# Gate logits from split values in 96 stacked rows, and the last four mixing steps of block B in the last two ticks of the dense layer of block A

## The reference, cut to what matters

```python
h = rmsnorm(x, p['norm_mix_g'])
z = jnp.einsum('btd,de->bte', h, p['w_in'])          # D_IN columns, 16 of them are glr
gq, gk, gv, gg, glr, dq, dk, dv = jnp.split(z, _split_points(), axis=-1)
gate_logit = jnp.einsum('btr,rk->btk', glr, p['w_gk2']) + p['b_gk']
log_a = (jax.nn.log_sigmoid(gate_logit) / GK_NORMALIZER).reshape(B, T, H_GLA, DK_GLA)
...
mix = jnp.concatenate([o_g.reshape(B, T, -1), o_d.reshape(B, T, -1)], axis=-1)
x = x + jnp.einsum('bte,ed->btd', mix, p['w_out'])
h2 = rmsnorm(x, p['norm_ffn_g'])
u = jnp.square(jax.nn.relu(jnp.einsum('btd,df->btf', h2, p['w_up'])))
x = x + jnp.einsum('btf,fd->btd', u, p['w_down'])
```

## Time and profile before

| | |
|---|---|
| median of 3 runs | 1342.72 us (1342.07 to 1342.86) |
| the profiled execution, its own time | 1342.28 us |
| span of the profiled execution | 1340.1 us |
| TensorE matmul busy | 1331.6 us, 99% |
| VectorE busy | 896.2 us, 67% |
| ScalarE busy | 577.6 us, 43% |
| GpSimd busy | 395.8 us, 30% |
| granted TensorE clock | 1.0 as the mean of the span |

### The profile page before, as it was taken

One profiled execution on the slowest core, in us unless ns is written; L12 is line 12 of the kernel. 1 busy time (PEld: TensorE's weight loads), 2 busy tenths in 40 slices (PEclk: granted clock), 3 DMA queues, 4 the chain that ended last, 5 costly groups with the idle time before them and its releaser, 6 DMA issues.

```text
span 1340.1 us, 23935 instructions
## 1 busy us (share of the span) xinstructions
PE 1331.6 (99%) x8605; PEld 1123.7 (84%) x8605; DVE 896.2 (67%) x1619; ACT 577.6 (43%) x1078; POOL 395.8 (30%) x397
## 2 busy tenths in 40 slices
PE   9999999999999999999999999999999999999999
PEld 8788888777777777887777777677999999999998
DVE  6479667846757776767666674444566665887785
ACT  7464333425645563631424342232454354434532
POOL 3648434455515434341000000000522210332030
PEclk9999999999999999999999999999999999999999
DMA  9458744454365565676658565881665465133301
GB/s 330 125 182 227 238 144 139 141 173 132 98 202 191 179 213 171 215 253 219 236 181 300 181 240 177 294 285 69 213 206 185 162 220 174 48 111 111 111 33 64
DMA packets 126135, 240.33 MB, mean 179 GB/s; under 512 B 13673, under 2 KB 47258, under 8 KB 126018
## 3 DMA queue, kind: packets, MB, share of 16 engines
q1 hardware_dynamic: 116802, 214.68, 48.8%
q10 hardware_dynamic: 9216, 24.14, 5.4%
HBM read 198.16 MB, written 40.62 MB: 178 GB/s over the span
## 4 chain that ended last, share of the span: by engine, by line
PE 96%; DVE 3%; ACT 1%; issue 1%; ACTq 0%; POOL 0%; DVEq 0%; POOLq 0%
PE ps L87 26%; PE ps L89 25%; PE ps L88 25%; PE ps L1576 3%; PE ps L1613 2%; PE ps L1396 2%; PE ps L3424 2%; PE ps L1597 1%; PE ps L428 1%; PE ps L1811 1%; PE ps L490 1%; PE ps L491 1%; PE ps L1437 1%; PE ps L1438 1%; PE ps L452 1%
## 5 line engine op out<-in xcount | busy, mean ns | idle before, releaser
L3182 POOL TENSOR_TENSOR kr<-kr,qb 128x512 f32<-128x512 f32 x128 | 174.3, 1370 | 161.9 <-DVE sd L3167 110.5
L87 PE MATMUL ps<-x2hB,uw_h 128*128 128x264 f32 (+1 forms) x512 | 145.1, 283 | 0.1
L88 PE MATMUL ps<-x2lB,uw_h 128*128 128x264 f32 (+1 forms) x512 | 144.7, 283 | 0.0
L89 PE MATMUL ps<-x2hB,uw_l 128*128 128x264 f32 (+1 forms) x512 | 144.5, 282 | 0.0
L87 PE MATMUL ps<-part_h,fh 128*128 128x264 f32 (+1 forms) x448 | 127.8, 285 | 0.0
L89 PE MATMUL ps<-part_h,fl 128*128 128x264 f32 (+1 forms) x448 | 127.1, 284 | 0.0
L88 PE MATMUL ps<-part_l,fh 128*128 128x264 f32 (+1 forms) x448 | 126.9, 283 | 0.0
L2948 DVE TENSOR_TENSOR xt<-xt,ps 128x264 f32<-128x264 f32 (+1 forms) x224 | 87.4, 422 | 35.8 <-PE ps L89 35.6
L3167 DVE TENSOR_REDUCE sd<-kr 128x8 f32<-128x512 f32 x128 | 85.4, 677 | 35.0 <-POOL kr L3182 35.0
L87 PE MATMUL ps<-uh,dh 128*128 128x512 f32 x256 | 104.1, 406 | 0.9 <-DVE xt L2255 0.8
L87 PE MATMUL ps<-x2hA,uw_h 128*128 128x512 f32 x256 | 104.5, 408 | 0.0
(11 more groups left out here) (395 smaller groups left out, 3406.6 us busy)
## 6 DMA issues: line engine op xcount, KB each, us to landing
kr<-in_cache_k SPq DMA_DIRECT2D x128, 256.0 KB, 3.1
raw_up<-in_w_up_units SPq DMA_DIRECT2D x64, 512.0 KB, 4.1
vr<-in_cache_v SPq DMA_DIRECT2D x128, 256.0 KB, 4.5
raw_dn<-in_w_down SPq DMA_DIRECT2D x32, 512.0 KB, 6.1
raw_dn<-in_w_down ACTq DMA_DIRECT2D x32, 512.0 KB, 4.7
raw<-in_w_in_units SPq DMA_DIRECT2D x23, 512.0 KB, 5.5
raw_up<-in_w_out_units SPq DMA_DIRECT2D x16, 512.0 KB, 4.0
kept_up_low<-uw_l SPq DMA_DIRECT2D x14, 512.0 KB, 6.4
```

Of the source, the lines that this page charges most:

```text
L87: pe.matmul(out, lh, rh, start=first and n == 0, stop=False, skip_group_check=onto)
L88: pe.matmul(out, lh, rl, start=False, stop=False, skip_group_check=onto)
L89: ins = pe.matmul(out, ll, rh, start=False, stop=last and n == len(ks) - 1, skip_group_check=onto)
L3182: pool.tensor_tensor(k[:, :], k[:, :], qb[v // PAGES][:, :], ALU.mult).then_inc(k_multiplied, 1)
```

## The change

Two things are changed.

1. **The gate logits.** `low` becomes a tile of its own, 96 rows of type fp32r at the address of `dg`, whose rows 96 to 127 now take the 32 rows that `low_rank` makes. ScalarE (`low_highs`, at the end of group 11) copies the high part of these rows into rows 0 to 31 and 64 to 95 of `low`, and the high part of `wgk` into rows 0 to 31 and 32 to 63 of a new tile `wgk_r`: eight copies. VectorE (`low_lows`, in group 12, behind the low parts of weight pieces 8 and 9) makes rows 64 to 95 of `wgk_r` and rows 32 to 63 of `low`: four subtractions. One fp32r matmul over the 96 rows gives high by high, high by low and low by high at once, in place of one float32 matmul over 128 rows. Each of the six now waits for the low part of its own piece. Two small memsets on GpSimd and one wait of SyncE go.
2. **The mixing.** The last four steps of block B's mixing are put at ticks 142, 142, 143 and 143.

```diff
-    low = dg
+    low = at("low", 170.6875, [96, NT], FP32R)
+    wgk_r = at("wgk_r", 4.75, [96, 256], FP32R)
...
-                sp.wait_ge(sem("pool_steps"), 8)
                 sp.wait_ge(gcol_in, 16)
                 for i in range(2):
-                    sp.dma_start(m["wgk"][16 * i:16 * (i + 1), :], a["w_gk2"]).then_inc(gcol_in, 16)
+                    sp.dma_start(m["wgk"][96 + 16 * i:112 + 16 * i, :], a["w_gk2"]).then_inc(gcol_in, 16)
...
+            if g == START["low"] + 2:
+                low_highs(act)
...
-            step.note(pool.memset(low[:, SEQ:NT], 0.0))
...
-            step.note(pool.memset(m["wgk"][:, :], 0.0))
...
-            dve.tensor_tensor(low[0:32, c0:c0 + n], ps[0:32, bank_of(g), 0:n], rb[0:32, c0:c0 + n], ALU.mult)\
+            dve.tensor_tensor(dg[96:P, c0:c0 + n], ps[0:32, bank_of(g), 0:n], rb[0:32, c0:c0 + n], ALU.mult)\
...
-            units_first = g in (START["gv"] - 3, START["dk"] + NTILE)
+            units_first = g in (START["low"] + 3, START["gv"] - 3, START["dk"] + NTILE)
             if not units_first:
                 beside(TICK[g])
             for r in split_after(g):
                 if r != 11:
                     split_low(r)
+            if g == START["low"] + 3:
+                low_lows(dve)
...
+    def low_highs(act):
+        act.wait_ge(gcol_in, 48)
+        for r in (0, 32):
+            ins = act.activation(wgk_r[r:r + 32, :], m["wgk"][96:P, :], ACT.Copy)
+        ins.then_inc(low_high, 1)
+        for c in range(3):
+            act.wait_ge(low_made, c + 1)
+            if c == 0:
+                act.wait_ge(r_spread, 2)
+            for r in (0, 64):
+                ins = act.activation(low[r:r + 32, columns(c)], dg[96:P, columns(c)], ACT.Copy)
+            ins.then_inc(low_high, 1)
+
+    def low_lows(dve):
+        dve.wait_ge(low_high, 2)
+        dve.tensor_tensor(wgk_r[64:96, :], m["wgk"][96:P, :], wgk_r[0:32, :].bitcast(FP32), ALU.subtract).then_inc(low_low, 1)
+        for c in range(3):
+            dve.wait_ge(low_high, 3 + c)
+            dve.tensor_tensor(low[32:64, columns(c)], dg[96:P, columns(c)], low[0:32, columns(c)].bitcast(FP32), ALU.subtract)\
+                .then_inc(low_low, 1)
...
-                pe.wait_ge(low_made, 3)
+                pe.wait_ge(low_low, 3 + c)
                 if i == 0:
                     pe.wait_ge(rb_made, 2)
-                    pe.wait_ge(diag_made, NTILE + 1)
-                    pe.wait_ge(gcol_in, 48)
...
-                pe.matmul(ps[:, logit_bank(i), 0:n], m["wgk"][:, mt * P:(mt + 1) * P], low[:, blk * HALF + off:blk * HALF + off + n],
+                pe.matmul(ps[:, logit_bank(i), 0:n], wgk_r[:, mt * P:(mt + 1) * P], low[:, columns(c)],
...
         put("mixB", [t0 + 137 + i // 2 for i in range(9)])
+        put("mixB", [t0 + 142, t0 + 142, t0 + 143, t0 + 143])
```

More of the change, by code:

```diff
@@ L999, in vector, with columns @@
                 m["late"]["vector"](dve, g - START["gg"] - 3)
+    def columns(c):
+        blk, off, n = PIECES[c]
+        return slice(blk * HALF + off, blk * HALF + off + n)
+    def low_highs(act):
[17 more added lines that the diff above has]
+                .then_inc(low_low, 1)
     def logit_bank(i):
```

## The result

| | kernel before | changed kernel |
|---|---|---|
| median of 5 runs | 1342.25 us (1342.07 to 1342.86) | 1350.1 us (1347.7 to 1350.96) |
| ratio, 95% interval | 1 | 1.0052 (1.004 to 1.0063) |
| profiled execution | 1342.28 us, span 1340.1 us | 1350.37 us, span 1348.2 us |
| mean granted clock of TensorE | 1.0 | 0.996 |

The forecast was 1345.6 us with 1343.6 to 1348.2 us around it. The direction was right. The size was not: some 8 us were lost, where the sum had 2.9.

A forecast was written before the change was run, and what follows sets the result against it. TensorE's work laid end to end was taken to bound the kernel: 1342.28 - 2.54 (logits) + 5.10 (first wait) + 0.1 (first matmul behind it) + 0.2 (transpose) = 1345.14 us profiled, 1345.6 us as median, range 1343.6 to 1348.2 us.

The forecast's parts named there:

- the sum: Whole profiled execution: 1342.28 - 2.54 + 5.10 + 0.1 + 0.2 = 1345.14 us; as a median 1345.6 us, 2.9 us slower.
- What TensorE no longer does is won in full: Whole span: TensorE's work lies end to end, with 1.6 us of waits, so saved work shortens the time fully.
- rival (a): Behind the first-logit wait TensorE's clock falls to half: 0.9 to 1.8 us more, 1347.1 us; chance 0.28.
- The place and length of the first wait: First gate logit: TensorE waits for VectorE's second subtraction and starts at 85.30 us, 5.10 us late.
- The turn: Shared port at 83.1 us: waiting GpSimd's key product goes first, so VectorE's first subtraction waits for 84.26 us.
- Rival (c): Weight piece 9 lands later, lengthening the first-logit wait by up to 1.6 us: 1347.2 us; chance 0.10.
- The matmul savings: Six gate logits: fp32r matmuls in place of float32 products save TensorE 2 x (0.63 + 0.31 + 0.33) = 2.54 us.
- ScalarE's copies: Eight copies between high parts of pieces 7 and 8 end by 79.2 us, hidden in idle time, costing nothing.
- GpSimd and the shared port: At the first logit's subtractions, VectorE and GpSimd exclude each other: wait 5.1 us, or 4.0 us if independent.
- Rival (b): GpSimd doesn't stand in the subtractions' way; TensorE starts the first logit 4.01 us late: 1344.5 us; chance 0.13.
- Part 2: Moved mixing at block A's dense layer end: transpose of `acc_s` ahead of output 7 costs 0.2 us (0.1 to 0.5).

The follow-up runs named there:

- lows_first: Changed kernel with VectorE's four logit subtractions ahead of the low parts of weight pieces 8 and 9: 1342.53 us, ratio 0.9998.
- gq_first: Changed kernel without the mixing change, subtractions ahead of low parts of pieces 8 and 9, six gq pieces ahead of their ticks' other work: 1342.49 us.
- lows_half_sums: Changed kernel, subtractions ahead of low parts of pieces 8 and 9, first 33 key sums over half of each head's columns: 1341.04 us, ratio 0.9984.
- after_half_sums: Changed kernel with VectorE's first 33 key sums over half of each head's columns: 1348.35 us, ratio 1.004.
- keys_later: Changed kernel with the key products and sums beginning two ticks later: 1351.94 us, ratio 1.0073.
- after_again: The changed kernel unedited, run again on one chip beside the repeat of another run: 1351.54 us, ratio 1.0054.
- piece_first: Changed kernel with VectorE's L918 of group 19 ahead of that tick's running sums and key sums: 1350.37 us, ratio 1.0057.
- piece_first_again: The kernel of piece_first unedited, run again beside the changed kernel on one chip: 1349.27 us, ratio 1.0048.
- busy_wait: Changed kernel with 21 extra matmuls, results unread, on TensorE ahead of its wait for the first logit's operands: 1346.65 us, ratio 1.0033.
- only_mixing: Kernel before with only the last four mixing steps at ticks 142, 142, 143, 143: 1342.70 us, ratio 1.0002.
- lows_between: Changed kernel with the four subtractions between the low parts of pieces 8 and 9: 1345.58 us (1343.54 to 1348.41), ratio 1.002.
- forced_wait: Kernel before, where TensorE's first logit also waits for the low part of weight piece 9: 1347.16 us (1345.44 to 1349.71), ratio 1.0038.
- before_half_sums: Kernel before with VectorE's first 33 key sums over half of each head's columns, the control: 1342.02 us, ratio 0.9994.

## Why the prediction was wrong, point by point

- **"What TensorE no longer does is won in full": this step failed.** It was read from the waits alone. The earlier trace rows says that TensorE hardly waits; it doesn't say by how much the other engines are in time. At 120.43 us VectorE was in time by less than 0.1 us. A TensorE that no longer needs 2.5 us meets a VectorE with nothing to spare. In the changed kernel VectorE's L918 was 7.15 us late, and the 1.9 us that TensorE had won back by 108.7 us became a wait of 2.2 us. lows_first shows it without the first wait (2.5 us saved, a wait of 2.1 us), gq_first with the next waits in line; in lows_half_sums and after_half_sums, with less work for VectorE, the wait shrinks to 0.5 us and to none. In the profile of the changed kernel the step was worth 2.2 us of wait and 1.6 us of clock, 3.8 of the 5.2 us by which the profiled execution missed the sum (1350.37 against 1345.14 us).
- **The sum also put the clock behind the first wait at nothing: 2.3 us.** It stood as rival (a) only; see below.
- **The place and length of the first wait: right.** TensorE started at 85.33 us, forecast 85.30 us. Piece 9's low part ended at 83.16 us, forecast 83.12; the second subtraction at 85.27 us, forecast 85.16. (The first was forecast to end at 84.55 us; 84.26 + 0.54 - 0.27 is 84.53, which changes nothing.) The turn went a little otherwise: the key product began at 83.27 us, so the first subtraction passed (0.42 us) and the second was blocked. keys_later shows that the product is the cause. That the forecast hit to 0.03 us is partly luck: TensorE was 0.25 us behind ahead of the logit before the change could act on it, and in five profiles of this wait it was 4.7, 5.7, 5.7, 5.9 and 6.0 us; in the longer ones piece 9 or the products had moved. Rival (c) had up to 1.6 us for a late landing.
- **Rival (a), the clock: it should have been the forecast.** It had 0.28, and the reason given was that no wait in the trace was near 5 us. But the earlier trace rows had the half clock behind a start at which TensorE had done nothing. The price worked out from them, 0.9 to 1.8 us, was too low: the half clock lasted 4.8 us behind the wait and not 3.6 us, and cost 2.3 us. In each of the six profiles with a first wait over 4 us and an idle TensorE the clock fell to 0.50 behind it (the changed kernel, after_again, piece_first, piece_first_again, keys_later and after_half_sums). busy_wait, with TensorE working through the wait, had none. The Trainium skill ("TensorE: Matmul & The Clock Gate", Part 1) has idleness bring the clock to half, and the trace agrees: 0.50 behind the 4.7 us wait. Had (a) been the forecast, 1347.1 us, it would still have been 3 us short, mostly by the second wait and the clock behind that.
- **The matmul savings: right in size.** The lag falls by 1.9 us from 90.15 to 108.7 us in the changed kernel, over the last five logits, for which the prediction has 2.54 - 0.63 = 1.9 us; in lows_first it falls by 2.5 us over all six, where 2.54 us were forecast.
- **ScalarE's copies: right.** They ran from 75.81 to 79.69 us, forecast to end by 79.2 us, and the high part of piece 9 began at 80.84 us against 80.80 us before.
- **GpSimd and the shared port: right.** The Trainium skill ("SBUF — State Buffer", "Who interferes with whom") has such a pair exclude each other for a whole instruction; the trace agrees with 1.63 us beside a product, and keys_later with 1.58 us for three without one. Rival (b) is out.
- **Part 2: right.** 0.2 us were forecast (0.1 to 0.5), and the profiles of the changed kernel and of only_mixing both show 0.12 us.
- **What stays open**: why the clock falls behind waits of 2.0 to 2.6 us in some executions (the changed kernel at 126 us, lows_between) and not in others (2.1 us in lows_first, 2.7 us in forced_wait). What share of VectorE's delay is luck in how its operations fall on GpSimd's was not tested either: no run takes the key products away from 100 to 130 us. And against its control lows_half_sums won 1.0 of the 2.5 us: that the rest is VectorE too is likely from its 19.6 of 20 us, and not shown.

The sum, had it been made with what the runs showed: 1342.28 - 2.54 (the saving) + 5.1 + 2.3 (first wait and clock) + 2.2 + 1.6 (second wait and clock) - 0.5 (what comes back later) = 1350.4 us.

## What to carry to other kernels

That an engine never waits doesn't mean that it may go faster: for each engine that hands it something, read how long before its use the thing was ready, above all in a stretch where that engine is busy for 99% of the time, and where its operations take longer if they fall beside another engine's. An operand that is made later than its turn in the order costs more than its wait if TensorE goes idle, because the clock can fall behind the wait, and because a partner engine that was only just in time can be the late one when TensorE catches up. Before changing what an operation costs, place the instructions that feed it ahead of whatever waits for a DMA: here a block of two lines moved up by three was worth more than 7 us (1350.1 to 1342.5 us).

## What the runs showed of the hardware

- TensorE's clock at half level behind a wait of 2.0 us at 125 to 127 us, until 3.5 us behind it, at a price of 1.6 us; and at full level behind waits of 2.1 us (lows_first) and 2.7 us (forced_wait). The length of one wait doesn't decide it.
- The clock at 0.50 from 620 to 622 us without any wait of TensorE and with 100% busy time, in one execution of before_half_sums, at a price of 1.6 us.
- Among ten runs of one kernel (lows_between) the time rises from 1343.5 to 1348.4 us as the mean granted clock falls from 1.0 to 0.997.
- A VectorE copy of 128 x 8 numbers takes 0.17 us in the kernel before where no key product is running (L1066 at 99.94 us), and 1.15 us where one is (L1066 at 117.06 us, L1091 at 123.17 us in the changed kernel): a tiny copy can cost nearly as much as the product that it stands behind. Halving the columns of a key sum brought it from 0.67 to 0.40 us only.
